# Half of an output projection by Strassen's seven products, in a fused attention block

## The reference, cut to what matters

```python
h = rms_norm(x, norm_in_w)                       # x: 512 tokens x 2048, float32
proj = h @ w_in
# mixer A: sliding-window attention with sinks; mixer B: latent attention,
# block-causal; each is multiplied by its SiLU gate
mixed = concatenate([out_a, out_b], axis=-1)     # 512 x 2048
x = x + mixed @ w_out                            # w_out: 2048 x 2048
return rms_norm(x, final_norm_w)
```

## Time and profile before

| what | us |
|---|---|
| time, median of 3 runs (673.65 to 673.66) | 673.66 |
| span of the profiled execution | 671.7 |
| PE busy in it | 664.6 (99%) |
| DVE busy | 332.3 (49%) |
| ACT busy | 309.1 (46%) |
| POOL busy | 306.7 (46%) |

### The profile page before, as it was taken

How to read it: one execution, slowest core, us unless ns; L and a number is a source line. 1 busy time by engine, 2 the same in 40 slices (tenths; PEclk the granted TensorE clock), 3 DMA queues, 4 the chain that set the end, 5 groups by cost and what they waited for, 6 DMA issues and landing times.

```text
span 671.7 us, 8933 instructions
## 1 busy us (share of the span) xinstructions
PE 664.6 (99%) x3187; PEld 559.0 (83%) x3187; DVE 332.3 (49%) x602; ACT 309.1 (46%) x593; POOL 306.7 (46%) x148
## 2 busy tenths in 40 slices
PE   9999999999999999999999999999999999999996
PEld 8888888888888888888888888888888888888885
DVE  6858132889684544654635668777651100101014
ACT  6833231311343753664564566867854321312234
POOL 0044443454244433433532526747866584474730
PEclk9999999999999999999999999999999999999999
DMA  8732322232222222212212313212024733222215
GB/s 298 274 115 91 108 94 95 83 105 95 94 94 95 79 79 95 94 63 95 95 63 94 126 44 118 71 53 96 32 92 174 281 123 114 94 94 95 93 45 237
DMA packets 22021, 73.54 MB, mean 109 GB/s; under 512 B 2400, under 2 KB 2656, under 8 KB 21856
## 3 DMA queue, kind: packets, MB, share of 16 engines
q1 hardware_dynamic: 18288, 65.81, 28.8%
q10 hardware_dynamic: 3696, 7.23, 2.9%
HBM read 68.83 MB, written 4.19 MB: 109 GB/s over the span
## 4 chain that ended last, share of the span: by engine, by line
PE 99%; ACT 0%; issue 0%; DVE 0%
PE bank L1149 30%; PE bank L1152 30%; PE bank L1153 30%; PE bank L1414 1%; PE bank L1293 1%; PE bank L1303 1%; PE bank L1179 1%; PE bank L1400 1%; PE bank L1401 1%; PE bank L1316 1%; PE bank L1315 1%; PE bank L1169 1%; PE bank L1172 1%; PE bank L1205 0%; PE bank L1212 0%; PE bank L1217 0%
## 5 line engine op out<-in xcount | busy, mean ns | idle before, releaser
L301 POOL TENSOR_TENSOR w_lo<-w_raw,w_hi 128x1024 fp32r<-128x1024 f32 x100 | 243.1, 2437 | 309.0 <-ACT w_hi L385 308.9
L385 ACT ACTIVATE w_hi<-w_raw 128x1024 fp32r<-128x1024 f32 x109 | 115.1, 1056 | 204.1 <-PE bank L1149 174.2
L1149 PE MATMUL bank<-x_hi,w_hi 128*128 128x512 f32 x496 | 193.7, 391 | 0.0
L1152 PE MATMUL bank<-x_hi,w_lo 128*128 128x512 f32 x496 | 193.3, 390 | 0.0
L1153 PE MATMUL bank<-x_lo,w_hi 128*128 128x512 f32 x496 | 193.2, 390 | 0.0
L1153 PEld LDWEIGHTS bank<-x_lo,w_hi 128*128 128x128 f32 x496 | 93.1, 188 | 19.7
L1149 PEld LDWEIGHTS bank<-x_hi,w_hi 128*128 128x128 f32 x496 | 93.2, 188 | 18.8 <-DVE mixed L947 0.2
L1152 PEld LDWEIGHTS bank<-x_hi,w_lo 128*128 128x128 f32 x496 | 93.2, 188 | 18.1
L1149 PE MATMUL bank<-w_hi,mx_hi 128*128 128x512 f32 (+1 forms) x260 | 100.9, 388 | 0.0
L1153 PE MATMUL bank<-w_lo,mx_hi 128*128 128x512 f32 (+1 forms) x260 | 100.4, 386 | 0.0
L1152 PE MATMUL bank<-w_hi,mx_lo 128*128 128x512 f32 (+1 forms) x260 | 100.4, 386 | 0.0
(11 more groups left out here) (236 smaller groups left out, 933.2 us busy)
## 6 DMA issues: line engine op xcount, KB each, us to landing
w_raw<-w_stream SPq DMA_DIRECT2D x109, 512.0 KB, 3.3
...
out<-y SPq DMA_DIRECT2D x6, 512.0 KB, 3.4
xs<-x_t SPq DMA_DIRECT2D x4, 512.0 KB, 5.2
mixed<-x_t SPq DMA_DIRECT2D x4, 512.0 KB, 5.2
...
out<-y SPq DMA_DIRECT2D x3, 256.0 KB, 2.4
xs<-w_stream SPq DMA_DIRECT2D x1, 512.0 KB, 3.4
```

The source lines that it names most:

```text
L301: pool.tensor_tensor(w_lo[:, s % HL, :], w_raw[:, s % RAW, :], w_hi[:, s % HL, :].bitcast(F32), ALU.subtract)\
L385: act.activation(w_hi[:, s % HL, :], w_raw[:, s % RAW, :], ACT.Copy).then_inc(w_hi_ready, 1)
L1149: ins = pe.matmul(dst, ah, bh, start=start, stop=False)
L1152: pe.matmul(dst, al, bh, start=False, stop=False)
```

## The change

Column blocks 0 and 1 stay as they are. For blocks 2 and 3 the product of `mixed` and the right half of `w_out` is done by Strassen's seven products. The 2 x 2 split is: tokens (a token tile of each pair q), rows of `w_out` (chunks of 128 in pairs), and the two column blocks. Seven products of (128 tokens, two pairs q) x (128 rows) x (512 columns) stand where eight stood.

- A pair of row blocks and both column blocks is one visit's data: 128 x 4 x 512 float32, 1 MB. There are 16 visits: in visits 0 to 7 three products are made with the data of pair v, in visits 8 to 15 the other four, with the same weights again in another order (`laid_out_pairs`; 16 MB in all where 8 MB were loaded). A visit is 18 matmuls in the first half and 24 in the second.
- DVE makes sums or differences of the weight blocks in place (`part_sums`), ACT high parts (`part_high`) in two groups g, and low parts are made of group 0 by POOL (`part_low(v)`, from visit 2) and of group 1 by DVE (`part_low(v, 1)`).
- Two raw buffers `t_raw[v % 2]` of 1 MB. SP loads visit v when both low parts of visit v - 2 are made.
- Sums of `mixed` blocks for the products are made, split and put away in the stage before (`unit_sums`, `unit_high`, `unit_low`; `pair_sums`, `pair_high`, `pair_low`).
- Products are in eight banks; DVE adds or subtracts each into `y` (`add`) after visit 7 and after visit 15. The final gain and the normalisation are arranged anew for that, without the short path of the last 256 columns.

The diff, cut to its core (the order of the `mixed` sums on each engine, the reordered finish on ACT and the data layout are left out):

```diff
-CHUNKS = WO0 + 32
+CHUNKS = WO0 + 16
+VISITS, PART = 16, 512
+TILES_DONE = (1, 0, 3, 2)
...
+        t_raw = [at("t_raw0", [P, 4, PART], F32, r_x + 56 * KB), at("t_raw1", [P, 4, PART], F32, r_raw)]
+        t_hi = [at(f"t_hi{par}", [P, 4, PART], F32R, r_hi + 8 * KB * (1 - par)) for par in range(2)]
+        t_lo = [at(f"t_lo{par}", [P, 4, PART], F32R, r_lo + 8 * KB * (1 - par)) for par in range(2)]
...
+        def part_slots(v, g):
+            return slice(0, 2) if g == 1 else slice(3, 4) if v < 8 else slice(2, 4)
...
-            for t in range(TOK - 1):
-                sp.wait_ge(o_scaled_act, t + 1)
+            sp.wait_ge(w_lo_ready, WO0 + 16)
+            sp.dma_start(t_raw[1][:, :, :], w_pairs[1, :, :, :]).then_inc(t_landed[1], 16)
+            for v in range(2, VISITS):
+                sp.wait_ge(t_low[0], v - 1)
+                sp.wait_ge(t_low[1], v - 1)
+                sp.dma_start(t_raw[v % 2][:, :, :], w_pairs[v, :, :, :]).then_inc(t_landed[v % 2], 16)
...
+            def part_low(v):
+                pool.wait_ge(t_high, 2 * v + 1)
+                s = part_slots(v, 0)
+                pool.tensor_tensor(t_lo[v % 2][:, s, :], t_raw[v % 2][:, s, :], t_hi[v % 2][:, s, :].bitcast(F32), ALU.subtract).then_inc(t_low[0], 1)
+            for v in range(2, VISITS):
+                part_low(v)
+                if v == 3:
+                    pool.wait_ge(fws_landed, 48)
+                if 4 <= v < 8:
+                    pool.wait_ge(o_squared, v + 2)
+                    gained(v - 4, 1)
+                if v == 12:
+                    for q in range(2):
+                        pool.wait_ge(o_squared, 8 + q + 2)
+                        gained(2 * q + 1, 2)
+            for q in range(2):
+                pool.wait_ge(o_squared, 11 + 3 * q + 2)
+                gained(2 * q, 3)
 
...
+            residual_in(0, y0_landed)
+            act.dma_start(t_raw[0][:, :, :], w_pairs[0, :, :, :]).then_inc(t_landed[0], 16)
+            residual_in(1, y1_landed)
+            act.dma_start(fw[0][:, :], final_w[:, 0:SEQ]).then_inc(fw_landed, 16)
             mixed_high(7)
...
+            def part_high(v, g):
+                if g == 0 and v < 8:
+                    act.wait_ge(t_landed[v % 2], 16 * (v // 2) + 16)
+                else:
+                    act.wait_ge(t_summed, v + 1 if v < 8 else 2 * v - 6 - (g == 1))
+                if v == 0:
+                    act.wait_ge(w_used, WO0 + 14)
+                elif v == 1:
+                    act.wait_ge(o_done, 8)
+                elif v < 9:
+                    act.wait_ge(t_used, 2 * v - 3 + g)
+                elif v == 9:
+                    act.wait_ge(m_done, 6 if g else 2)
+                else:
+                    act.wait_ge(t_used, 2 * v - 5 + g)
+                s = part_slots(v, g)
+                act.activation(t_hi[v % 2][:, s, :], t_raw[v % 2][:, s, :], ACT.Copy).then_inc(t_high, 1)
 
...
+            act.wait_ge(u_low, 8)
+            residual_in(2, y_landed)
+            residual_in(3, y_landed)
+            part_high(1, 0)
+            pair_high(7)
+            part_high(1, 1)
+            act.wait_ge(p_low, 8)
+            for n in range(1, 4):
+                act.dma_start(fw[n][:, :], final_w[:, SEQ * n:SEQ * n + SEQ]).then_inc(fws_landed, 16)
+            for t in range(TOK):
+                act.wait_ge(o_evac, 4 + t + 5)
+                square(t, 1, 4 + t)
+            for v in range(2, VISITS):
+                part_high(v, 0)
+                part_high(v, 1)
+                if v == 10:
+                    for q in range(2):
+                        act.wait_ge(y_added, 7 + q)
+                        square(2 * q + 1, 2, 8 + q)
...
+            def unit_sums(j):
+                if j >= 2:
+                    dve.wait_ge(u_low, j - 1)
+                even, odd = by_tile(mixed, 2 * j), by_tile(mixed, 2 * j + 1)
+                for n, (a, b) in enumerate(((even[:, :, 0, :], odd[:, :, 1, :]), (even[:, :, 1, :], odd[:, :, 1, :]), (even[:, :, 0, :], odd[:, :, 0, :]))):
+                    dve.tensor_tensor(u_sum[j % 2][:, n, :].rearrange("p (q c) -> p q c", q=2), a, b, ALU.add).then_inc(u_summed, 1)
+            def unit_low(j):
+                dve.wait_ge(u_high, j + 1)
+                dve.tensor_tensor(u_lo[j][:, :, :], u_sum[j % 2][:, :, :], u_hi[j][:, :, :].bitcast(F32), ALU.subtract).then_inc(u_low, 1)
+            def pair_sums(j):
+                if j < 7:
+                    dve.wait_ge(w_used, WO0 + 9 + j)
+                else:
+                    dve.wait_ge(o_done, 8)
+                if j >= 2:
+                    dve.wait_ge(p_low, j - 1)
+                even, odd = by_tile(mixed, 2 * j), by_tile(mixed, 2 * j + 1)
+                dve.tensor_tensor(p_sum[:, j % 2, 0, :, :], even[:, :, 1, :], even[:, :, 0, :], ALU.subtract).then_inc(p_summed, 1)
+                dve.tensor_tensor(p_sum[:, j % 2, 1, :, :], odd[:, :, 0, :], odd[:, :, 1, :], ALU.subtract).then_inc(p_summed, 1)
+            def pair_low(j):
+                dve.wait_ge(p_high, j + 1)
+                dve.tensor_tensor(dead(mx_lo[j]), p_sum[:, j % 2, :, :, :], dead(mx_hi[j]).bitcast(F32), ALU.subtract).then_inc(p_low, 1)
+            def part_sums(v):
+                raw = t_raw[v % 2]
+                dve.wait_ge(t_landed[v % 2], 16 * (v // 2) + 16)
+                dve.tensor_tensor(raw[:, 0:2, :], raw[:, 0:2, :], raw[:, 2:4, :], ALU.subtract if v < 8 else ALU.add).then_inc(t_summed, 1)
+                if v >= 8:
+                    dve.wait_ge(t_summed, 2 * v - 7)
+                    dve.tensor_tensor(raw[:, 2, :], raw[:, 2, :], raw[:, 3, :], ALU.add).then_inc(t_summed, 1)
+            def part_low(v, g):
+                dve.wait_ge(t_high, 2 * v + g + 1)
+                s = part_slots(v, g)
+                dve.tensor_tensor(t_lo[v % 2][:, s, :], t_raw[v % 2][:, s, :], t_hi[v % 2][:, s, :].bitcast(F32), ALU.subtract).then_inc(t_low[g], 1)
...
+            def add(t, n, bk, done, after=0, op=ALU.add):
+                dve.wait_ge(m_done, done)
+                if after:
+                    dve.wait_ge(y_added, after)
+                ys = y[:, t, SEQ * n:SEQ * n + SEQ]
+                dve.tensor_tensor(ys, ys, B[bk][:, :], op).then_inc(y_added, 1)
...
+            for t in range(TOK):
+                residual(1, t)
+            pair_sums(7)
+            part_low(1, 0)
+            pair_low(7)
+            part_sums(2)
+            part_low(1, 1)
+            for v in range(2, 9):
+                part_sums(v + 1)
+                part_low(v, 1)
+            dve.wait_ge(y_landed, 32)
+            for q in range(2):
+                add(2 * q + 1, 2, 4 + q, q + 1)
+                add(2 * q + 1, 3, 4 + q, q + 1, op=ALU.subtract)
+            for q in range(2):
+                add(2 * q, 3, 6 + q, q + 3)
+            for q in range(2):
+                add(2 * q + 1, 2, q, q + 5, 2 * q + 1)
+            part_low(9, 1)
+            part_sums(10)
+            for v in range(10, VISITS):
+                if v < VISITS - 1:
+                    part_sums(v + 1)
+                part_low(v, 1)
...
+            def m(v, q, bk, s, slot, start=False):
+                return three(B[bk + q][:, :], *s, t_hi[v % 2][:, slot, :], t_lo[v % 2][:, slot, :], start, v in (7, 15), goes_on=v >= 8 and bk in (0, 6))
...
+            for v in range(8):
+                pe.wait_ge(t_low[0], v + 1)
+                pe.wait_ge(u_low, v + 1)
+                if v == 0:
+                    pe.wait_ge(b_probs, 32)
+                for q in range(2):
+                    ins = m(v, q, 4, s2(v, q), 3, v == 0)
+                    if v == 7:
+                        ins.then_inc(m_done, 1)
+                if v < 7:
+                    ins.then_inc(t_used, 1)
+                pe.wait_ge(t_low[1], v + 1)
+                if v == 0:
+                    pe.wait_ge(b_out, 9)
+                for q in range(2):
+                    ins = m(v, q, 6, s_kept(v, q, 0, 0), 0, v == 0)
+                    if v == 7:
+                        ins.then_inc(m_done, 1)
+                if v == 0:
+                    pe.wait_ge(o_evac, 10)
+                for q in range(2):
+                    ins = m(v, q, 0, s_kept(v, q, 1, 1), 1, v == 0)
+                    if v == 7:
+                        ins.then_inc(m_done, 1)
+                if v < 7:
+                    ins.then_inc(t_used, 1)
...
+            for q in range(2):
+                pe.wait_ge(t_low[0], 15)
+                m1(14, q)
+                pe.wait_ge(t_low[0], 16)
+                m1(15, q).then_inc(m_done, 1)
+                pe.wait_ge(t_low[1], 16)
+                pe.wait_ge(p_low, 8)
+                m6(14, q)
+                m6(15, q).then_inc(m_done, 1)
+                m5(14, q)
+                m5(15, q).then_inc(m_done, 1)
+                m7(14, q)
+                m7(15, q).then_inc(m_done, 1)
 
```

(35 more changed lines are left out.)

329 lines of the change are left out of this document (191 added, 138 removed).

## The result

The changed kernel takes 720.69 us, the median of 4 runs (719.64 to 721.71), beside 673.65 us before (673.60 to 673.66): a ratio of 1.070, interval 1.0685 to 1.0715. It is slower by 47 us. The forecast was 727.4 with a range from 708 to 740.

What follows compares the result with a forecast made beforehand. TensorE, busy 99%, bounds the kernel before; after, load, sums and low part run in series. Visit 15's low part at 700.4, then 19.9 on DVE and 5.1 for the store: span 725.4, time 727.4, range 708 to 740.

Steps and rivals of the forecast that it cites:

- the third rival: POOL and DVE don't hinder each other in the visits, at the end or before the visits: 713.5 us; chance 20%.
- L(1): End of DVE's group 1 low part of visit 1: 583.8 without lag, 5 us of lag taken, so 588.8.
- The first load: First load in the sum, before visit 3's sums, meets 0.75 MB of gains: up to 2.3 us, taken 1.0.
- Visits 3 to 6: Load 5.0, sums 1.2, POOL 1.3 and low part 1.2 in series: 8.7 us a visit.
- The additions between the blocks: DVE's 8 additions out of the banks, 5.5 us, and a low part: visit 9's low part ends 6.8 later.
- Visits 10 to 14: Load, both sums and low part in series, 8.1 us a visit: 40.5 us for five.
- TensorE's end: After DVE's last low part TensorE still has 14 triples of matmuls, 9.5 us, ending at 709.9.
- The finish: After the last low part: DVE's additions, normalisation and waits for ACT, 19.9 us, then the last store, 5.1.
- TensorE stays the bound: Rival for the whole kernel: loads hide under matmuls, finish 2 to 3 us longer, 665.3 us; chance 3%.
- loads overlap: Rival for the visits: DVE's next low part does not stand behind the load, time 689 us; chance 4%.
- The long load: Rival for the visits: each load takes 5.5 us, with 3 us more lag before them, 736.4 us; chance 12%.
- the signs named ahead: Expected profile: DVE idle some 5 us per load, TensorE waiting some 4.6 then 2.7 us, one load at a time.

Runs made afterwards that it cites:

- e1: Changed kernel with DVE making visit v's low part before visit v + 1's sums, from visit 2 on: 695.51 us, ratio 1.0334.
- e3: Changed kernel with ACT's group 0 high part in visits 3 to 7 waiting for DVE's sums, so POOL's input comes later: 714.84 us, ratio 1.0617.
- e7: Changed kernel with one of the three matmuls of each product left out in visits 2 to 13: 720.84 us, ratio 1.0717.
- e6: Changed kernel with low part before sums, all low parts on DVE, group 1 first in visits 9 to 14, residual and gain loads later: 686.47 us.
- e8: Changed kernel with low part before sums, all low parts on DVE, up to four raw buffers, loads, additions and squares reordered: 681.22 us, ratio 1.0135.

## Why the prediction was right

The mechanism was the forecast's: one load, the sums and the low part in series in each visit, POOL within them up to visit 7. e1, e3 and e7 changed one thing each and moved the time by what it says (-25.2, -5.9, none). By the time alone it would not be told from a rival: 720.7 is 6.7 us under the forecast and 7.2 over the third rival's 713.5. It is e3 that decides. The span came out at 717.5, not 725.4; step by step, with L(v) the end of DVE's low part:

- **L(1).** 585.07, not 588.8. The bound without lag was 583.8; 5 us of lag was taken "nearer the upper end", and 1.3 came. With -3.7 us this is the largest term that was mis-sized. The reason given for it, that the work of both engines fills the stretch, was wrong. DVE did meet POOL: between 541 and 563 six rows are 11.5 us longer in sum than the same instructions alone (the first row below: three sums that take 1.09 us elsewhere), more than the 8 of the upper bound. But POOL was done at 562.4 and stood idle to 588.02, and DVE had caught up before its last residual additions. So L(1) came early by a pause of POOL that the forecast did not see. That the bounds of this term held was luck.

```profile
547.83 4.38 DVE L1196 TENSOR_TENSOR u_sum<-mixed 128x256 f32<-128x256 f32 x3
...
588.02 1.26 POOL L405 TENSOR_TENSOR t_lo<-t_raw,t_hi 128x512 fp32r<-128x512 f32 x1 [25.60 <-ACT t_hi L717]
```

- **The first load.** L(2) is 11.17 us later, not 9.7. DVE waited 7.73 where other visits have 4.8, so the loads in the way cost 2.9, not 1.0. The forecast counted the gains' 0.75 MB alone; ACT had also issued the residual's last 2 MB at 578.38, 6.8 us before this load was issued, and the residual's loads of 1 MB landed after 6.1 us (median of four).
- **Visits 3 to 6.** L(2) to L(6) are 33.1 us, 8.27 a visit, not 8.7. The wait for the load is 4.73 to 4.95 (taken 5.0), the sums 1.14 to the next start, the low part 2.3 with POOL's 1.08 (taken 1.3). L(6) to L(8): 15.7, not 16.2.
- **The additions between the blocks.** Eight took 4.87, not 5.5, and L(9) came after 5.92, not 6.8.
- **Visits 10 to 14.** 40.4 us, predicted 40.5, and L(15) 3.45, predicted 3.6. So L(15) is 694.75, not 700.4.
- **TensorE's end.** 11.05 us behind that, not 9.5. The forecast had every matmul at 0.227 apart. In fact the first ones after the last wait came 0.43 apart (last section), and DVE and ACT, not TensorE, still ended last.
- **The finish.** 22.75 from L(15), not 25.0. DVE's last scaling ended at 713.17, 18.4 after L(15) and not 19.9, so 4.3 for the store, not 5.1. DVE's last scaling and the issue of the last store:

```profile
712.69 0.48 DVE L1317 TENSOR_SCALAR y<-y,fin 128x512 f32<-128x512 f32 x1
...
713.57 0.43 SPq L320 DMA_DIRECT2D out<-y  x1
```

The terms up to L(15) are 5.6 us less in sum and the finish 2.3 less: 7.9, the whole miss of the span.

Of the rivals, the first, that TensorE stays the bound, is excluded by its 37.0 us of waiting in the two blocks. That loads overlap needed the other order; e1, which has it, gained 25 us, though not the 38 that this rival gave, since DVE then waits for ACT and TensorE for POOL. That POOL and DVE don't hinder each other was the nearest of the rivals in time (713.5) and is wrong in mechanism: the low part lasted 2.3 and e3 took 5.9 away. The long load, 5.5 us, is excluded by waits of 4.73 to 4.97.

The fit of the Trainium skill (DMA: Bandwidth & Descriptors, Anatomy of one DMA) gave an estimate of 4.4 us for 1 MB; the skill states it for DMAs issued by GpSimd, and these are issued by SyncE. The profile page of the changed kernel has 4.8, which is what the rate of the earlier trace rows gave. The time of about 722 that followed from the skill's figure was nearer to 720.7 by luck: what made the time shorter was the lag before the visits, and not the load.

Of the signs named ahead, two came in part only. DVE sat idle for a load in every visit but one: the sums of visit 10 did not wait, as its load landed under the additions. TensorE was said to stand 4.6 us before each second product up to visit 7 and some 2.7 after. Up to visit 7 it stood 5.3 us in visit 2 and then 1.3 to 3.8 in turn, since slower matmuls filled part of the visit. From visit 8 on it stood before the second product in three visits only (1.82, 2.12 and 0.59), besides 4.6 for DVE's additions in visit 8 and 6.7 for POOL's low part of visit 15: having lost time in visit 8, it still had work left when the low parts of the next visits were ready.

What stays open: how much the longer finish (5.7 us) costs by itself, since no run changed it alone; why 512 KB out of a wider row landed in 3.7 us and a contiguous 512 KB in 3.3; what cost more in e6, the moved loads or the moved gains; and whether a version without the waits of e8 would beat the kernel before by the 4.8 us estimated.
